# Split products for all wide input projections: halves of the activations kept, weights through two pairs of buffers

## The chip, the cores and the metric

One core of one Trainium2 chip runs the kernel. The metric is device time in microseconds, the median of several runs. The core has five engines: PE (matmul; its weight loads are shown apart as PEld), DVE (vector), ACT (scalar), POOL (GpSimd) and SP, which here only issues transfers.

## What is computed

One decoder layer on 512 tokens of width 1024, float32. Cut to what matters here:

```python
h = rmsnorm(x, g_pre_mix) * (1.0 + scale_m) + shift_m      # 512 x 1024
proj = h @ w_in                                            # one wide product, split by columns:
(gq, gk, gv, gg, ga_low, dq, dk, dv, iq, ik, iw, bg) = jnp.split(proj, offsets, axis=-1)
# widths 256 256 512 512 16 512 512 512 512 64 8 2048
o_a = gla_chunked(...gq, gk, gv, decay(ga_low)...)         # gated linear attention, silu(gg) on its output
o_b = dsa_attention(dq, dk, dv, top-128 keys by iq, ik, iw)
mix = sigmoid(bg[0]) * (o_a @ w_proj_gla) + sigmoid(bg[1]) * (o_b @ w_proj_dsa)
x   = x + gate_m * rmsnorm(mix @ w_out)
x   = x + gate_f * rmsnorm(hier_moe(h2))                   # 32 experts, top 2 of one group
```

## The kernel before, in words

The tokens lie in four tiles of 128 (`tt`), the width in eight blocks of 128 (`KD`). `hT` holds the transposed activations h in SBUF (8 blocks of 128 x 512). Each wide weight item is a block of 512 output columns, 2 MB, 128 x 4096 in SBUF. The list `items` gives their order: four `ada` items (conditioning), then IQ (index query), DK, DQ, DV, GQ (query and key of the linear attention, made transposed), GV, GG, BG, BG+D, proj 0, BG+512, BG+D+512, proj 1, out 0, out 1. SP loads them in that order (`load(n)`), into a ring of four buffers, item n once item n-4 is used up (with a few exceptions written out); PE counts used items in `ring_out`.

A product of one item and one token tile (`inproj`, L463) is eight fp32 matmuls of 128x512 into a PSUM bank A0 or A1; the trace records each as two instructions, so a product is sixteen. DK, the two proj items, BG+512, BG+D+512 and the two out items run already as split products (`inproj_split`, `split_matmul`, L471 to L473): ACT copies the float32 source to its high half in fp32r (`split_hi`, L1186), DVE subtracts to get the low half (`split_lo`, L1624), and PE does high x high, high x low and low x high, 24 matmuls for a product. The halves of h are made twice: once at the start for DK, into kv (high), gqk and qT (low), which are then overwritten (L1200, L1629), and once at the end of attention (`split_hi("h")`, L1832) for the late items. IQ, DQ, DV, GQ, GV, GG, BG and BG+D run in fp32 from `hT`.

Every engine works through its own list in program order, with semaphores between them:
- Start: `ada(0)`, then the narrow products `small` (L526, 88 columns) for four tiles, then IQ and DK, each with one `ada_step` (1 MB of conditioning weights through ACT's queue) per tile.
- Index stage, twelve steps n: PE does `index_scores(n)`; ACT the relu; DVE adds it up (L1686, L1688) and then does four rounds of the top-128 search (`some(4)`, L1664, L1665). In steps 3 to 6 and 8 to 11 PE also does one product each, of DQ and of DV.
- Attention stage, units u = 0 to 16: PE does `attn_scores(u)`, one product (GQ in u 0 to 3, GV, GG, BG four units each), and `attn_out(u-1)`: transposes (L592), ACT copies one half of them (L1347), DVE the other (L1821), and PE multiplies (L601). DVE masks the scores (L1797), in units 0 to 3 also finishes the search, and normalizes (L1806, L1807); ACT does the exponentials (L1332). From u = 8 on, the linear attention of chunk ch runs over an even unit (POOL L1066, DVE `gla_clamp` L1729, ACT `gla_exp` L1307 to L1311, DVE `gla_factors` L1736 and L1741, `gla_take` L1782, PE `gla_scores`) and the odd unit after it (PE `gla_out`, DVE `gla_norm` L1774).
- Then BG+D, `branches(0)`, BG+512, BG+D+512, `branches(1)`, the output product with the router, and 16 pairs of experts, whose weights SP loads into three sets of buffers.

Of the kernel before, what the change touches and what calls it, by code (L numbers as in the profile page):

```python
# [24 lines left out]
P = 128  # L25
# [55 lines left out]
def layer(nc, x, c, positions, w_ada, b_ada, g_pre_mix, g_post_mix, g_pre_ffn, g_post_ffn, w_in,  # L81
# [17 lines left out]
    with ExitStack() as ctx:  # L99
# [10 lines left out]
        def sem(name):  # L110
# [4 lines left out]
        ring = arena[:, 0:4 * 4096].rearrange("p (s n) -> p s n", s=4)  # L115
        hT = arena[:, 16384:20480].rearrange("p (k n) -> p k n", k=KD)
        prob = arena[:, 20480:22528].rearrange("p (b h n) -> p b h n", b=2, h=2)
        probT = arena[:, 22528:24576].rearrange("p (b h n) -> p b h n", b=2, h=2)
        adab = arena[:, 20480:24576].rearrange("p (b n) -> p b n", b=2)
        yc = arena[:, 0:8192].rearrange("p (t w n) -> p t w n", t=TT, w=2)  # L120
        wexp = arena[:, :].rearrange("p (s n) -> p s n", s=4)
# [6 lines left out]
        kv = sb("kv", [P, 4096])  # L128
        kT = kv[:, 0:2048].rearrange("p (c n) -> p c n", c=PAIRS)
# [25 lines left out]
        diag = stage_mem[:, 0:D]  # L155
        gla_mem = sb("gla_mem", [P, 3072])
# [78 lines left out]
        area_r["G"] = gvs_r[:, :]  # L235
        g_all, q_all = (v[:, :, :].rearrange("p a n -> p (a n)") for v in (gqk, qT))
        splits = {key: (area[raw], area_r[lo], area_r[hi]) for key, raw, lo, hi in (
            (("in", O_DK), 1, 1, 3), ("h", "H", "G", "B"), (("proj", 0), 1, 1, 3), (("in", O_BG + 512), 2, 2, "H"), (("in", O_BG + D + 512), 0, 0, 3),
            (("proj", 1), 1, 1, 2), (("out", 0), "H", "H", "B"), (("out", 1), 3, 3, "G"))}
        splits["g"], splits["q"] = (g_all, gqk_r[:, :], qi_r), (q_all, qT_r[:, :], stage_r)  # L240

        h_first = ([gqk_r[:, P * TT * k:P * TT * (k + 1)] for k in range(4)] + [qT_r[:, P * TT * k:P * TT * (k + 1)] for k in range(4)],
                   kv_r[:, :].rearrange("p (k n) -> p k n", k=KD))
        split_at = {key: n for n, key in enumerate(["h_first", ("in", O_DK), "h", ("proj", 0), "g", "q", ("in", O_BG + 512), ("in", O_BG + D + 512),
                                                    ("proj", 1), ("out", 0), ("out", 1)])}
# [17 lines left out]
        gu_sets = [[wexp[:, 2 * z + q, 0:4096] for q in range(2)] for z in range(2)] + [[gvs[:, :], qs_mem[:, :]]]  # L263
        down_sets = [[wexp[:, 2 * z + q, 4096:6144] for q in range(2)] for z in range(2)] + [[mk_mem[:, :], gla_mem[:, 0:2048]]]
# [91 lines left out]
        def slot_of(it):  # L356
            if it in splits:
                return splits[it][0]
            return ring[:, item_at[it] % 4, :]
# [15 lines left out]
        def _(pe):  # L375
# [52 lines left out]
            def ada_step(m):  # L428
# [7 lines left out]
                for j in range(4):  # L436
                    last = nc.tensor.matmul(o[32 * j:32 * j + 32, :], c32[:, k, :], adab[:, m % 2, j * 512:(j + 1) * 512],  # L437
                                            start=(k == 0), stop=(k == KD - 1))
# [16 lines left out]
            def inproj(it, tt):  # L455
# [6 lines left out]
                for k in range(KD):  # L462
                    last = nc.tensor.matmul(a[:, :], hT[:, k, tt * P:(tt + 1) * P], w[:, k, :], start=(k == 0), stop=(k == KD - 1))  # L463
# [11 lines left out]
            def split_wait(key):  # L475
                pe.wait_ge(hi_ready, split_at[key] + 1)
                pe.wait_ge(lo_ready, split_at[key] + 1)

            def inproj_split(it, tt):
                first = it == ("in", O_DK)  # L480
                split_wait("h_first" if first else "h")
                split_wait(it)
                w = parts(it, KD)

                def h(k):
                    hi, lo = (h_first[1][:, k, :], h_first[0][k]) if first else (v[:, k, :] for v in parts("h", KD))
                    return hi[:, tt * P:(tt + 1) * P], lo[:, tt * P:(tt + 1) * P]

                a, full = take_next("A", (it, tt))
                for k in range(KD):  # L490
                    last = split_matmul(a[:, :], h(k), [v[:, k, :] for v in w], k == 0, k == KD - 1)
                last.then_inc(full, 1)
                if tt == TT - 1:
                    pe.wait_ge(full, bank[where[(it, tt)]].at[(it, tt)] + 1)
                    pe.sem_inc(ring_out, 1)

            def inproj_T(it, cb):

                ring_wait(pe, it)
                a, full = take_next("A", (it, cb))  # L500
                w = slot_of(it).rearrange("p (k n) -> p k n", k=KD)
                for k in range(KD):
                    last = nc.tensor.matmul(a[:, :], w[:, k, cb * P:(cb + 1) * P], hT[:, k, :], start=(k == 0), stop=(k == KD - 1))  # L503
# [15 lines left out]

            pe.wait_ge(ld_small, 32)  # L520
            for tt in range(TT):
                a, full = take_next("A", ("small", tt))
                for k in range(KD):
                    if tt == 0:
                        pe.wait_ge(h_ready, k + 1)
                    last = nc.tensor.matmul(a[:, 0:NS], hT[:, k, tt * P:(tt + 1) * P], w_small[:, k, :], start=(k == 0), stop=(k == KD - 1))  # L526
                last.then_inc(full, 1)
            for tt in range(TT):
                inproj(("in", O_IQ), tt)
                ada_step(tt)  # L530
# [362 lines left out]
        def _(sp):  # L893
# [27 lines left out]
            for n in range(4):  # L921
                load(n)
            sp.dma_start(w_small[:, :, 0:RANK], win_v[:, :, O_GA:O_GA + RANK]).then_inc(ld_small, 16)
            sp.dma_start(w_small[:, :, RANK:NS], win_v[:, :, O_IK:O_IK + 72]).then_inc(ld_small, 16)
            load(4)
            load(5)
# [27 lines left out]

            sp.wait_ge(ring_out, item_at[("proj", 1)] + 1)
            experts(0, 0, 1)
# [4 lines left out]

            gate_up(2, 0, 4)
            down(2, 0, 4)
            sp.wait_ge(x1_ready, 2 * TT)
            gate_up(2, 1, 5)
# [182 lines left out]
        def _(act):  # L1148
# [34 lines left out]
            def split_hi(key):  # L1183

                src, _, hi = splits[key]
                nc.scalar.copy(hi, src).then_inc(hi_ready, 1)  # L1186


            def ada_load(m):
                act.dma_start(adab[:, m % 2, :], ada_v[:, m % KD, (1 + m // KD) * 2048:(2 + m // KD) * 2048]).then_inc(ada_in[m % 2], 16)  # L1190
# [3 lines left out]
            for tt in range(TT):  # L1194
                a, free = filled(act, ("small", tt))
                nc.scalar.copy(ikw[:, tt, :], a[:, 0:NS]).then_inc(ikw_in, 1)
                act.wait_ge(ikw_in, tt + 1)
                act.sem_inc(free, 1)
            act.wait_ge(h_ready, KD)
            nc.scalar.copy(h_first[1], hT).then_inc(hi_ready, 1)  # L1200
            act.wait_ge(ring_out, 4)
# [32 lines left out]
            for tt in range(TT):  # L1234
                to_stage((("in", O_IQ), tt))
                ada_next(tt + 2)
            act.wait_ge(lnv_ready, 1)
            nc.scalar.activation(st[:, 56:60], st[:, 52:56], ACT.Sqrt).then_inc(lnq_ready, 1)
            for tt in range(TT):
# [24 lines left out]
            for n in range(3 * PAIRS):  # L1264
# [19 lines left out]
                if n in WITH_PRODUCT:  # L1284
                    fill.pop(0)()

# [26 lines left out]
            gscr = stage_mem[:, 0:P]  # L1313
# [10 lines left out]
            for u in range(NU + 1):  # L1324
# [15 lines left out]
                if u:  # L1340
# [3 lines left out]
                    t, free = filled(act, ("p", v, 0))  # L1344
                    if v >= 2:
# [8 lines left out]
                if not odd and 0 <= ch < TT:  # L1354
# [5 lines left out]
                    act.sem_inc(free, 1)  # L1360
            scratch = gla_mem[:, 0:D]


            split_hi("h")
            sigmoid(0, 1, 0)
            act.wait_ge(ring_out, item_at[("in", O_BG)] + 1)
# [12 lines left out]
            act.wait_ge(ring_out, item_at[("in", O_BG + D)] + 1)  # L1379
            act.wait_ge(lo_ready, split_at["h"] + 1)  # L1380
            ring_wait(act, ("in", O_BG + 512))
            split_hi(("in", O_BG + 512))
            for ab, (used, key) in enumerate(((("proj", 0), ("in", O_BG + D + 512)), (("in", O_BG + 512), ("proj", 1)))):
# [755 lines left out]
```

## Time and profile before

| | |
|---|---|
| median of three runs | 894.28 us (892.54 to 897.63) |
| the profiled execution | 895.17 us, its span 893.4 us |
| PE busy | 760.0 us (85%), 3251 instructions |
| PEld, DVE, ACT, POOL busy | 408.1, 347.3, 257.7, 100.5 us |
| chain that ended last | PE 73%, DVE 11%, issue 7%, DMA 5%, ACT 3% |
| mean granted TensorE clock | 0.926 of 2.4 GHz |

A share of busy time says which engine has most to do over the whole span; the chain says what the end waited for, step by step. Both mix stages with different limits, so the rows below go stage by stage. In a table of stretches each row gives the length of the stretch, each engine's busy time (and number of instructions), the granted clock, the busy share of the DMA engines and GB/s. A line such as L1624 is the line of a helper that many steps share.

### The profile page before, as it was taken

Reading aid. Unit: us, or ns where it says so; the run is one execution under the profiler, and the core shown is the slowest. Engines: PE = TensorE matmul, PEld = TensorE weight load, DVE = VectorE, ACT = ScalarE, POOL = GpSimd, SP = SyncE. Lnnn points to the kernel's source line nnn. Section 1 sums busy time; section 2 is a strip of 40 time slices with the busy share of each in tenths; the row PEclk is TensorE's granted clock in tenths of the full one; section 3 lists DMA queues with packets and bytes.
Section 4 is the critical chain, followed back from the end, with each engine's and each line's share of the span. In section 5 each row is a group of like instructions: output and inputs, shape, how many; then the busy total and the mean of one; then the engine's idle time right before and its main releaser. Section 6 shows DMA issues by size and latency. Waiting matters only on the chain.

```text
span 893.4 us, 9183 instructions
## 1 busy us (share of the span) xinstructions
PE 760.0 (85%) x3251; PEld 408.1 (46%) x3251; DVE 347.3 (39%) x820; ACT 257.7 (29%) x479; POOL 100.5 (11%) x153
## 2 busy tenths in 40 slices
PE   2899989998899998989999989976998787787840
PEld 1554624343344554554578768852333232232310
DVE  3241024699733444536421374761522111112117
ACT  5031121432223554645212312313122121112123
POOL 3022201310000210100000000101010100101004
PEclk9879979999999989999999999976999898999985
DMA  9954483307022002000222235169799999999734
GB/s 344 376 192 141 142 311 113 102 1 282 16 79 94 1 1 95 1 1 1 94 95 95 94 139 238 48 264 398 285 421 421 420 421 420 417 421 421 323 123 184
DMA packets 45563, 179.48 MB, mean 201 GB/s; under 512 B 9567, under 2 KB 9673, under 8 KB 30157
## 3 DMA queue, kind: packets, MB, share of 16 engines
q1 hardware_dynamic: 37124, 149.48, 42.4%
q10 hardware_dynamic: 3464, 20.98, 6.6%
q0 software_dynamic: 4928, 8.42, 2.7%
q8 instruction: 27, 0.44, 0.2%
q14 instruction: 20, 0.16, 0.1%
HBM read 174.66 MB, written 12.59 MB: 210 GB/s over the span
## 4 chain that ended last, share of the span: by engine, by line
PE 73%; DVE 11%; issue 7%; DMA 5%; ACT 3%; SPq 0%; ACTq 0%; DVEq 0%; POOLq 0%; PEldq 0%
PE psA L463 19%; PE psG L842 7%; PE psS L842 7%; PE psA L863 6%; PE psA L471 6%; PE psA L473 5%; PE psA L472 5%; PE psT L829 2%; PE psA L526 2%; PE psO L437 2%; PE psO L601 1%; DVE mk_mem L1665 1%; DVE m L1664 1%; PE psS L582 1%; DMA xn_dram<-sig_mem 1%
## 5 line engine op out<-in xcount | busy, mean ns | idle before, releaser
L463 PE MATMUL psA<-arena 128*128 128x512 f32 x448 | 202.7, 607 | 0.0
L463 PEld LDWEIGHTS psA<-arena 128*128 128x128 f32 x448 | 84.8, 194 | 110.2 <-issue 110.2
L842 PE MATMUL psS<-arena,kv 128*64 128x512 f32 x192 | 50.4, 685 | 14.7 <-issue 14.7
L842 PE MATMUL psG<-arena,kv 128*64 128x512 f32 x160 | 39.9, 654 | 7.5 <-issue 7.5
L863 PE MATMUL psA<-arena,sig_mem 128*64 128x512 f32 x176 | 40.7, 605 | 0.5 <-ACT sig_mem L1490 0.5
L2060 DVE TENSOR_TENSOR sig_mem<-sig_mem,psS 128x256 f32<-128x256 f32 x8 | 4.9, 614 | 92.6 <-ACT sig_mem L1485 92.4
L1112 POOL DMA_INDIRECT y_dram<-sig_mem,tables x16 | 16.0, 1003 | 208.1 <-issue 134.4
L842 PEld LDWEIGHTS psS<-arena,kv 128*64 128x64 f32 x192 | 17.1, 156 | 46.9 <-issue 46.9
L1624 DVE TENSOR_TENSOR arena_r<-arena,arena_r 128x4096 fp32r<-128x4096 f32 x6 | 26.5, 4421 | 30.8 <-ACT arena_r L1186 30.8
L472 PE MATMUL psA<-arena_r,qs_mem_r 128*128 128x512 f32 x96 | 37.4, 389 | 0.0
L471 PE MATMUL psA<-arena_r,qs_mem_r 128*128 128x512 f32 x80 | 31.8, 398 | 3.5 <-DVEq L1855 2.7
L2060 DVE TENSOR_TENSOR sig_mem<-sig_mem,psG 128x256 f32<-128x256 f32 x8 | 4.9, 615 | 75.4 <-ACT sig_mem L1485 75.3
L1289 ACT ACTIVATE sig_mem<-psA 128x512 f32<-128x512 f32 x16 | 9.6, 597 | 76.3 <-PE psA L473 52.8
L1433 ACT ACTIVATE kv<-psT,shift,scale 128x128 f32<-128x128 f32 x64 | 24.1, 456 | 22.1 <-PE psT L829 22.1
L503 PE MATMUL psA<-arena 128*128 128x512 f32 x64 | 29.6, 616 | 0.0
L1874 DVE TENSOR_SCALAR kv<-psT,scale,shift 128x128 f32<-128x128 f32 x64 | 21.9, 404 | 19.4 <-PE psT L829 17.4
L842 PEld LDWEIGHTS psG<-arena,kv 128*64 128x64 f32 x160 | 13.7, 150 | 32.4 <-issue 31.5
L1664 DVE MAX8 m<-mk_mem 128x8 f32<-128x256 f32 (+2 forms) x48 | 26.9, 560 | 1.5
L1485 ACT ACTIVATE sig_mem<-psS 128x256 f32<-128x256 f32 x8 | 3.1, 384 | 84.4 <-PE psS L842 84.4
L601 PE MATMUL psO<-arena,kv 128*64 128x128 f32 x160 | 16.0, 284 | 12.0 <-ACT arena L1347 8.5
L1665 DVE MATCH_REPLACE8 mk_mem<-m,mk_mem 128x256 f32<-128x256 f32 (+2 forms) x48 | 26.0, 542 | 0.0
L829 PE MATMUL psT<-ident,kv 128*128 128x128 f32 x128 | 18.5, 292 | 8.8 <-DMA kv<-xn_dram,tables 8.8
(394 smaller groups left out, 1368.0 us busy)
## 6 DMA issues: line engine op xcount, KB each, us to landing
arena<-in_w_in_dram SPq DMA_DIRECT2D x11, 2048.0 KB, 10.4
arena<-in_w_e_gate_dram SPq DMA_DIRECT2D x22, 1024.0 KB, 24.8
arena<-in_w_e_up_dram SPq DMA_DIRECT2D x22, 1024.0 KB, 26.8
arena<-in_w_e_down_dram SPq DMA_DIRECT2D x22, 1024.0 KB, 20.6
arena<-in_w_ada_dram ACTq DMA_DIRECT2D x16, 1024.0 KB, 4.9
arena<-in_w_ada_dram SPq DMA_DIRECT2D x4, 2048.0 KB, 17.0
gvs<-in_w_e_gate_dram SPq DMA_DIRECT2D x5, 1024.0 KB
gvs<-in_w_e_up_dram SPq DMA_DIRECT2D x5, 1024.0 KB
```

Source lines behind the costliest of these rows:

```text
L463: last = nc.tensor.matmul(a[:, :], hT[:, k, tt * P:(tt + 1) * P], w[:, k, :], start=(k == 0), stop=(k == KD - 1))
L471: nc.tensor.matmul(acc, lhs[0], rhs[0], start=start, stop=False)
L472: nc.tensor.matmul(acc, lhs[0], rhs[1], start=False, stop=False)
L473: return nc.tensor.matmul(acc, lhs[1], rhs[0], start=False, stop=stop)
L503: last = nc.tensor.matmul(a[:, :], w[:, k, cb * P:(cb + 1) * P], hT[:, k, :], start=(k == 0), stop=(k == KD - 1))
L601: last = nc.tensor.matmul(o[64 * hh:64 * hh + 64, 0:P], val[:, kb, (2 * hp + hh) * HD:(2 * hp + hh + 1) * HD], probT[:, u % 2, hh, kb * P: ...
L829: last = nc.tensor.transpose(ps[name][:, q * P:(q + 1) * P], xg[:, b, k * P:(k + 1) * P], ident[:, :])
L842: last = nc.tensor.matmul(ps[g][64 * q:64 * q + 64, :].rearrange("p (g f) -> p g f", g=2), h2g[:, b, k, 64 * q:64 * q + 64], gu, start=(k ...
L863: last = nc.tensor.matmul(ps[name][64 * q:64 * q + 64, :], actT[:, b, kf, 64 * q:64 * q + 64], down_sets[z][q][:, D * kf + 512 * n:D * kf ...
L1624: V.tensor_tensor(lo, src, hi, ALU.subtract).then_inc(lo_ready, 1)
L1664: step(V.max(m8[:, :], work))
L1665: step(V.match_replace(work, m8[:, :], work, TAKEN))
```

## The change

IQ stays in fp32; the other wide items (DQ, DV, GQ, GV, GG, BG, BG+D besides those split before) run as split products. Its parts:

1. **h.** The raw `hT` moves to kv. Its halves are made once, `split_hi("h")` and `split_lo("h")`, into areas H and B of the arena, and stay there until BG+D+512 is done. The second split of h and the copies of the first in gqk, qT and kv are gone.
2. **Weights.** Items go in turn through two pairs of areas, (0, 1) and (3, 2): the raw item and then its low half in the first, the high half in the second. `load(n)` waits for n-1, so for the item two places before, which had the same pair. IQ has area 2, the ada items have 0, 1, H and B. out 0 goes to H and B, out 1 to 0 and 1.
3. **Splits in quarters.** DV, GQ, GV, GG, BG and BG+D are split in four pieces of 128x1024, put into the lists of ACT and DVE: for DV after steps 4 to 7 of the index stage, for GQ after steps 9 to 11, for the other four over the four units before their first product (ACT one, two, one and no piece; DVE none, one, two, one, at the end of the unit). ACT waits for the item's load before its first piece. PE waits piece by piece in the item's first product. DQ is split whole, after the index key is ready.
4. **Start.** SP loads IQ and DK before the narrow weights `w_small`. PE does IQ and its ada steps first and `small` after them; ACT copies the narrow results after IQ.
5. **Places.** `prob` moves to stage_mem, `probT` to the upper half of sig_mem, the two buffers of `ada_step` to qT and the upper half of gvs; the first expert sets get other areas. The first expert's gate and up weights are loaded before proj 1 is used up, and `gate_up(2, 1, 5)` before the wait for x1.

```diff
-        splits = {key: (area[raw], area_r[lo], area_r[hi]) for key, raw, lo, hi in (
-            (("in", O_DK), 1, 1, 3), ("h", "H", "G", "B"), (("proj", 0), 1, 1, 3), ...
+        split_order = [("in", O_DK), ("in", O_DQ), ("in", O_DV), ("in", O_GQ), ("in", O_GV), ("in", O_GG), ("in", O_BG), ("in", O_BG + D),
+                       ("proj", 0), ("in", O_BG + 512), ("in", O_BG + D + 512), ("proj", 1), ("out", 0), ("out", 1)]
+        home = {key: ((0, 1), (3, 2))[n % 2] for n, key in enumerate(split_order)}
+        home[("out", 0)], home[("out", 1)] = ("H", "B"), (0, 1)
+        splits = {key: (area[lo], area_r[lo], area_r[hi]) for key, (lo, hi) in home.items()}
+        splits["h"] = (kv[:, :], area_r["H"], area_r["B"])
+        hi_units, lo_units = ((0,), (1, 2), (3,), ()), ((), (0,), (1, 2), (3,))
+        hi_index = {4: [(dv, 0)], 5: [(dv, 1), (dv, 2)], 6: [(dv, 3)], 9: [(gq, 0), (gq, 1)], 10: [(gq, 2), (gq, 3)]}
+        lo_index = {5: [(dv, 0)], 6: [(dv, 1), (dv, 2)], 7: [(dv, 3)], 10: [(gq, 0)], 11: [(gq, 1), (gq, 2), (gq, 3)]}
...
             def inproj_split(it, tt):
...
                 for k in range(KD):
-                    last = split_matmul(a[:, :], h(k), [v[:, k, :] for v in w], k == 0, k == KD - 1)
+                    if tt == 0 and k % 2 == 0:
+                        split_wait(it, k // 2 + 1)
+                    last = split_matmul(a[:, :], [v[:, k, tt * P:(tt + 1) * P] for v in h], [v[:, k, :] for v in w], k == 0, k == KD - 1)
...
+            for tt in range(TT):
+                inproj(("in", O_IQ), tt)
+                ada_step(tt)
             pe.wait_ge(ld_small, 32)
...
-                    sp.wait_ge(ring_out, {7: 6, 8: 7, 9: 8, 15: 13, 16: 14, 17: 15, 18: 16}.get(n, n - 3))
+                    sp.wait_ge(ring_out, {4: 1, 5: 2, 6: 3, 18: 16}.get(n, n - 1))
...
+                for q in hi_units[u % 4] if u < NU else ():      # ACT, end of unit u
+                    key = in_units[u // 4]
+                    if q == 0:
+                        ring_wait(act, key)
+                    split_hi(key, q)
...
+                for q in lo_units[u % 4] if u < NU else ():      # DVE, end of unit u
+                    split_lo(in_units[u // 4], q)
```

## Rows read from the trace of the kernel before

**Rows 1.** The page: the chain that ended last, by engine.
```profile
PE 73%; DVE 11%; issue 7%; DMA 5%; ACT 3%; SPq 0%; ACTq 0%; DVEq 0%; POOLq 0%; PEldq 0%
```

**Rows 2.** Stretches: length, busy us of each engine, clock, DMA share, GB/s.
```profile
131.20:169.30 38.10, 37.53 (x130) 15.48 (x128) 16.68 (x45) 12.79 (x19) 7.39 (x17) 1.00 0.30 100
169.30:224.40 55.10, 51.22 (x144) 22.64 (x144) 51.26 (x136) 15.25 (x30) 8.30 (x15) 1.00 0.43 148
224.40:245.10 20.70, 18.82 (x54) 8.62 (x54) 15.74 (x47) 4.23 (x14) 0.00 (x0) 0.92 0.04 7
245.10:284.40 39.30, 35.83 (x127) 16.71 (x126) 10.13 (x44) 9.91 (x29) 0.00 (x0) 1.00 0.17 60
284.40:406.40 122.00, 112.09 (x575) 62.68 (x574) 56.69 (x168) 66.69 (x134) 15.32 (x17) 0.96 0.09 32
595.50:893.40 297.90, 215.91 (x967) 84.59 (x966) 72.78 (x164) 60.16 (x136) 41.72 (x36) 0.86 0.88 360
```

**Rows 3.** The chain of waits in order of time: start, us, what.
```profile
300.02 7.08 PE psA L463 x16
406.52 27.48 PE psA L463 x64
```

**Rows 4.** Order of time, ACT: copies behind split products in a row.
```profile
469.72 0.60 ACT L1289 ACTIVATE sig_mem<-psA 128x512 f32<-128x512 f32 x1 [1.04 <-PE psA L473]
475.16 0.60 ACT L1289 ACTIVATE sig_mem<-psA 128x512 f32<-128x512 f32 x1 [4.84 <-PE psA L473]
```

**Rows 5.** Groups by shape: busy us, mean ns, idle before. Whole splits.
```profile
L1186 ACT CAST arena_r<-arena 128x4096 fp32r<-128x4096 f32 x7 | 25.4, 3622 | 1.0 <-ACT sig_mem L1289 0.9
L1624 DVE TENSOR_TENSOR arena_r<-arena,arena_r 128x4096 fp32r<-128x4096 f32 x6 | 26.5, 4421 | 30.8 <-ACT arena_r L1186 30.8
```

**Rows 6.** Order of time, SP's queue at the start.
```profile
27.74 3.31 SPq L913 DMA_DIRECT2D arena<-in_w_in_dram  x2
```

**Rows 7.** Transfers issued from 27.0 to 28.6 us: KB, us to landing.
```profile
arena<-in_w_in_dram SPq DMA_DIRECT2D x1, 2048.0 KB, 10.9
```

**Rows 8.** The chain of waits: narrow products, first IQ, router products.
```profile
35.60 14.07 PE psA L526 x64
49.67 9.01 PE psA L463 x16
569.05 1.71 PE psG L741 x16
```

**Rows 9.** Stretches of one microsecond, columns as in Rows 2.
```profile
36.00:37.00 1.00, 1.00 (x6) 0.68 (x5) 1.00 (x3) 0.00 (x0) 0.00 (x0) 0.86 1.07 403
53.00:54.00 1.00, 1.00 (x3) 0.48 (x2) 0.30 (x1) 1.00 (x2) 0.00 (x0) 0.60 0.15 55
```

**Rows 10.** Order of time, DVE: the ends of a stretch without gaps.
```profile
169.37 1.30 DVE L1688 SCALAR_TENSOR_TENSOR mk_mem<-gqk,wi,mk_mem 128x384 f32<-128x384 f32 x2 [4.61 <-ACT gqk L1273]
...
224.10 0.28 DVE L1821 COPY arena<-psT 128x128 f32<-128x128 f32 x1
```

**Rows 11.** The chain of waits in an even unit and the odd one behind.
```profile
317.80 0.67 DVE gqk L1782
329.56 9.15 PE psA L463 x16
```

**Rows 12.** Order of time, ACT and DVE, beginning of that even unit.
```profile
309.79 1.28 ACT L1332 ACT_TABLE_LOAD   x1
310.26 0.56 DVE L1797 CUSTOM_DVE_ANT_0 arena<-psS,mk_mem 128x384 f32<-128x384 f32 x1 [1.93 <-PE psS L582]
311.17 0.61 ACT L1332 ACTIVATE arena<-arena,sm 128x384 f32<-128x384 f32 x1
```

**Rows 13.** Line L913: transfers of w_in, eleven issues.
```profile
DMA to landing us min/median/max: 7.6/10.4/20.4
```

**Rows 14.** Order of time, DVE, in the first branches products.
```profile
441.69 4.42 DVE L1624 TENSOR_TENSOR arena_r<-arena,arena_r 128x4096 fp32r<-128x4096 f32 x1
446.02 0.68 DVE L1854 TENSOR_TENSOR sig_mem<-psA,sig_mem 128x512 f32<-128x512 f32 x1
```

More of the change, by code:

```diff
@@ L497, in inproj_T @@
             def inproj_T(it, cb):
-                ring_wait(pe, it)
+                w, h = parts(it, KD), parts("h", KD)
                 a, full = take_next("A", (it, cb))
-                w = slot_of(it).rearrange("p (k n) -> p k n", k=KD)
                 for k in range(KD):
-                    last = nc.tensor.matmul(a[:, :], w[:, k, cb * P:(cb + 1) * P], hT[:, k, :], start=(k == 0), stop=(k == KD - 1))
+                    if cb == 0 and k % 2 == 0:
+                        split_wait(it, k // 2 + 1)
+                    last = split_matmul(a[:, :], [v[:, k, cb * P:(cb + 1) * P] for v in w], [v[:, k, :] for v in h], k == 0, k == KD - 1)
                 last.then_inc(full, 1)
@@ L952, in experts @@
                 down(z, 1, e1_)
+            gate_up(0, 0, 0)
             sp.wait_ge(ring_out, item_at[("proj", 1)] + 1)
-            experts(0, 0, 1)
+            gate_up(0, 1, 1)
+            down(0, 0, 0)
+            down(0, 1, 1)
             sp.wait_ge(ring_out, len(items))
@@ L1181, in _, with split_hi @@
             mod_row(0)
-            def split_hi(key):
+            def split_hi(key, q=None):
                 src, _, hi = splits[key]
-                nc.scalar.copy(hi, src).then_inc(hi_ready, 1)
+                part = slice(None) if q is None else slice(1024 * q, 1024 * (q + 1))
+                nc.scalar.copy(hi[:, part], src[:, part]).then_inc(hi_ready, 4 if q is None else 1)
             def ada_load(m):
-                act.dma_start(adab[:, m % 2, :], ada_v[:, m % KD, (1 + m // KD) * 2048:(2 + m // KD) * 2048]).then_inc(ada_in[m % 2], 16)
+                act.dma_start(adab[m % 2], ada_v[:, m % KD, (1 + m // KD) * 2048:(2 + m // KD) * 2048]).then_inc(ada_in[m % 2], 16)
             for m in range(2):
                 ada_load(m)
[L1194 to L1198, printed above, removed]
+            act.wait_ge(ring_out, 4)
             act.wait_ge(h_ready, KD)
-            nc.scalar.copy(h_first[1], hT).then_inc(hi_ready, 1)
-            act.wait_ge(ring_out, 4)
+            split_hi("h")
             ring_wait(act, ("in", O_DK))
@@ L1236, in _ @@
                 ada_next(tt + 2)
+            for tt in range(TT):
+                a, free = filled(act, ("small", tt))
+                nc.scalar.copy(ikw[:, tt, :], a[:, 0:NS]).then_inc(ikw_in, 1)
+                act.wait_ge(ikw_in, tt + 1)
+                act.sem_inc(free, 1)
             act.wait_ge(lnv_ready, 1)
             nc.scalar.activation(st[:, 56:60], st[:, 52:56], ACT.Sqrt).then_inc(lnq_ready, 1)
+            act.wait_ge(ring_out, item_at[("in", O_IQ)] + 1)
+            ring_wait(act, ("in", O_DQ))
+            split_hi(("in", O_DQ))
+            act.wait_ge(lo_ready, split_at["h"] + 4)
             for tt in range(TT):
@@ L1377, in _ @@
             sigmoid(0, 1, 3)
-            act.wait_ge(ring_out, item_at[("in", O_BG + D)] + 1)
-            act.wait_ge(lo_ready, split_at["h"] + 1)
             ring_wait(act, ("in", O_BG + 512))
             split_hi(("in", O_BG + 512))
-            for ab, (used, key) in enumerate(((("proj", 0), ("in", O_BG + D + 512)), (("in", O_BG + 512), ("proj", 1)))):
+            for ab, key in enumerate((("in", O_BG + D + 512), ("proj", 1))):
                 sigmoid(1, ab, 0)
-                act.wait_ge(ring_out, item_at[used] + 1)
                 ring_wait(act, key)
@@ L1716, in _ @@
                     mod_take(1 + n // 10)
+                for key, q in lo_index.get(n, ()):
+                    split_lo(key, q)
             dve.wait_ge(ld_ffn, 16 * 5)
```

98 lines of the change are left out of this document (40 added, 58 removed).

## The prediction

> **What bounds the kernel now.** I read the page first: the chain that ended last is PE for 73% of the span and DVE for 11% [rows 1]. That says only that PE is the usual bound, so I cut the span into stretches [rows 2] and asked of each which engine has no room. From 131.2 to 169.3 us (index stage, DQ) PE is busy 37.5 of 38.1 us: PE binds. From 169.3 to 224.4 (DV, first GQ) PE is busy 51.2 of 55.1 us, but DVE 51.3, and in order of time its instructions follow each other from 169.37 to 224.10 with nothing but the small steps between them [rows 10]: both are at their limit. From 224.4 to 245.1 DVE is busy 15.7 of 20.7. From 245.1 to 284.4 DVE has only 10.1 of 39.3: PE alone. From 284.4 to 406.4 no engine is full by itself; there the chain of waits goes around through DVE and ACT [rows 11]. From 406.4 PE runs BG+D without a gap [rows 3]. From 595.5 on the experts run with the DMA engines at 0.88 and 360 GB/s; nothing there changes in amount, so I take the end as moving with the start of that stretch.
>
> **One product.** In fp32 it is 7.08 us between other work and 27.48/4 = 6.87 in a row [rows 3]. A split product in a row takes 475.16 - 469.72 = 5.44 us [rows 4]; with other work between I take 5.51. So a product gains 1.57 us, or 1.43 in a row, at the full clock. Seven items of four products change: 28 x 1.57 = 44 us if nothing else limits. The split costs per item 3.62 us on ACT and 4.42 on DVE [rows 5]; in quarters I estimate 1.0 and 1.1 us. DVE's sum is 7 x 4.42 = 31 us, less some 4.4 us for the h split now made once, and it is what decides, stage by stage.
>
> **Start.** Before, the narrow products took 14.07 us at 35.60 and then IQ began with 9.01 us [rows 8], because the clock had gone to half at 36 us and came back only at 53 [rows 9]. The same kind of narrow product at the full clock is 1.71/16 = 107 ns each (router), against 14.07/64 = 220. IQ was issued at 27.74 and took 10.9 us, to 38.6 [rows 6, 7], behind the narrow weights; with those behind it I take it to land at about 36.3, bounds 35 to 38.6. IQ's dense work then sits at half clock and brings it back, and `small` after it runs at the full clock: 64 x 107 ns = 6.9 us. Gain 14.07 - 6.9 - 0.7 for the later IQ = 6.5 us, bounds 0 (all narrow products at half clock again) and 8.5 (the clock does not fall at all). The halves of h and DK need ACT twice 3.62 and DVE twice 4.42 us; they are ready near 54 us, and PE wants them near 77: hidden. So is DQ's split (8 us behind the narrow results, with over 30 us until its first product). If that cover went, each would cost its 8 us.
>
> **Index stage and units 0 to 3.** PE's four DQ products give 4 x 1.57 = 6.3 us, and DVE can follow, with its 16.7 busy of 38.1 us [rows 2] and three more pieces (3.3): its gapless run starts 5.8 us earlier in relation to DQ. From there DVE sets the pace: before, 169.4 to 245.1 is 75.7 us with 3.4 us of waiting; without the waiting and with nine pieces more (one of DV after step 7, four of GQ after steps 10 and 11, four of GV after units 1 to 3), 72.3 + 9.9 = 82.2 us, 6.5 more. Net loss 0.7, say 1 us: the 4 x 1.57 of DQ and also the eight products of DV and GQ are eaten. Bounds: +19 if the pieces found room (12 x 1.57), -5 if DVE also kept its old waits. PE's wait for a piece of DV or GQ falls into time in which it would wait for DVE anyway.
>
> **Units 4 to 7.** DVE 10.1 us of 39.3 plus four pieces, ACT 9.9 plus four: room. 4 x 1.57 = 6.3 us gained.
>
> **Units 8 to 15.** In the even unit u = 10 DVE's mask starts at 310.26, with PE's product [rows 12]; clamp, ACT's exponentials and DVE's factors follow, and `gla_take`, which frees the bank for PE, ends at 317.80 + 0.67 [rows 11]: 8.2 us, more than the 7.08 of the product beside it. So shortening that product gains nothing in units 10, 12 and 14; unit 8, which has no `gla_take`, gives 0.5. Worse, ACT has two pieces (2.1 us) at the end of units 9 and 13, ahead of the next unit's table load of 1.28 us at 309.79 and the exponential at 311.17, which had no room between them [rows 12]: +1.9 us each. Behind that waiting ACT are the factors, and behind them PE's transposes. In the odd units PE's product ends the unit, after DVE's normalizing: 4 x 1.57 = 6.3. DVE's own pieces at the end of units 9, 11, 13 and 15 (1.1 us each) fit into the 1.93 us that it waits ahead of the mask [rows 12], those of 10 and 14 under `gla_out`. Sum 6.3 + 0.5 - 3.8 = +3.0, bounds -4 and +13.
>
> **BG+D:** 4 x 1.43 = 5.7 us gained, in a row and with its pieces ready.
>
> **First branches.** BG+512 now may load only when BG+D is used up, at T. The shortest load is 7.6 us [rows 13]: T+7.7, ACT to T+11.4, DVE to T+15.9. DVE has that split in its list before `mixing(0,1)`, which frees the bank for PE's fifth half-product. Before, the split ran at 441.69 and the mixing at 446.02 [rows 14], which is T+12.0 with T = 434.0. Now it is T+15.9: 3.9 us lost, bounds 0 and 8 (load of 11.5). The loads of BG+D+512, proj 1, out 0 and out 1 have four products or more before them (21.8 us against 16): 0. The two places where expert weights come earlier change nothing that the chain waits for: 0.
>
> **The clock.** PE now idles more where DVE or ACT leads. The odd unit at 329.56 shows what it costs: 9.15 us for a product of 7.08 [rows 11], with the clock at 0.96 over the whole of the linear attention [rows 2]. I take one and a half such events more: -3 us, bounds 0 and -17. By itself: the Trainium skill, TensorE: Matmul & The Clock Gate, section on HAM oscillation, says that waits between bursts of matmuls throw the clock back, so that each burst starts cold again; it speaks against this change, and by it the clock rival below would hold. The trace agrees in one place in four here.
>
> **Sum.** 6.5 - 1 + 6.3 + 3.0 + 5.7 - 3.9 - 3 = 13.6 us off the profiled execution's 895.17 (span 893.4 and 1.8 around it), so 881.6. The median of the runs stood 0.9 below that execution: 880.7, say 881.
>
> **The rivals.**
> - *DVE's pieces find room.* The pieces go where DVE waits, and DV and GQ gain too: 12 x 1.57 = 18.8 instead of -1, time 861. For it: DVE is idle 21 us between 131.2 and 169.3 [rows 2]. Against: only two and a half items' pieces could be put there, and the run from 169.4 has no gap.
> - *The clock.* Each of the eight units of linear attention loses the 2.07 us of the product at 329.56: 8 x 2.07 = 17 instead of 3, so 895. For: rows 11. Against: before, most of its units kept the full clock.
> - *ACT stands at a load (slower).* ACT waits for an item's load at the end of the unit after the pair came free. PE needs about 9 us to there, a load 7.6, so it just fits. The median landing is 10.4 and the longest 20.4 [rows 13]; from 9 us on ACT holds up its own exponentials, DVE behind them and PE. At 14 us, 5 us for each of GV, GG, BG, BG+D and 3 for BG+512, with the softmax chain restarted each time: 22 us, time 903. Against: after 171 us the DMA engines are nearly idle, 0.04 to 0.17 in units 1 to 16 [rows 2].
> - *The start gives nothing*, because the narrow products stay slow behind IQ: 887.5.
>
> **How the numbers follow.** Forecast as worked out 0.54; DVE finds room 0.13; clock 0.14; ACT at the loads 0.10; start 0.09. A measurement of this kernel tells 0.5% (4.5 us) from no change. Faster than 889.8: 0.54 + 0.13 + 0.09 and 0.01 of the clock case, 0.77; within: 0.12; slower: 0.11. Range 867 to 894: it leaves out the far ends of the first and third rivals.
>
> **What would show it.** Right: from DQ's first product to `attn_scores(4)` 115 us, about as before (245.1 - 131.2 = 113.9), with DVE busy over 90% and PE some 20 us less; units 4 to 7 near 7.9 us each; even units 10 and 14 longer than 12; PE's wait before its fifth half-product in `branches(0)` at about 5 us; narrow products near 7 us behind IQ. Wrong: narrow products at 14 us, clock under 0.9 in units 8 to 16, ACT idle for a DMA at the end of units 0, 4, 8 or 12, or a start of the experts that does not move the end.

## The result, and the profile after

The changed kernel takes 906.35 us (median of four runs: 902.3, 905.3, 907.4 and one of 1219.4 at a granted clock of 0.557, a slow run that the ratio leaves out) against 895.45 before. The ratio is 1.0124, 95% interval 1.0096 to 1.0151; on a second chip it was 1.0119 (1.0064 to 1.0174). The forecast was 881 us, with a range up to 894. It went the other way.

The page of the changed kernel (span 905.7, before 893.4): the chain that ended last, by engine. It answers to [rows 1].

```profile
PE 65%; DVE 15%; issue 8%; DMA 6%; ACT 5%; SPq 0%; ACTq 0%; DVEq 0%; POOLq 0%; PEldq 0%
```

Stretches of the changed kernel (length, busy us of PE, PE's loads, DVE, ACT, POOL, clock, DMA share, GB/s). The first three stand for the second to fourth of [rows 2], cut at nearly the same points of the program; 274.10:416.00 is units 8 to 15 with their tail; the last lies as the fifth of [rows 2] does.

```profile
157.10:217.20 60.10, 48.59 (x192) 34.84 (x192) 56.22 (x141) 20.00 (x35) 7.88 (x15) 0.88 0.18 55
218.00:239.10 21.10, 16.66 (x71) 12.40 (x70) 19.24 (x51) 7.08 (x17) 0.00 (x0) 0.82 0.18 61
239.10:274.10 35.00, 31.53 (x155) 23.56 (x154) 14.78 (x49) 13.52 (x32) 0.00 (x0) 0.94 0.09 28
274.10:416.00 141.90, 125.95 (x640) 93.50 (x640) 69.00 (x177) 72.89 (x142) 15.38 (x17) 0.76 0.12 44
284.40:406.40 122.00, 110.79 (x546) 82.76 (x544) 56.47 (x151) 64.48 (x125) 12.21 (x15) 0.72 0.05 18
```

In the last row, over the same 122 us, PE is as busy as before (110.8 us, 112.1 before), but at a mean clock of 0.72 instead of 0.96. PE's busy time hides it: work that has become shorter takes as long because more of it runs at half clock. Cut where the clock changes, units 8 to 15 of the changed kernel hold four stretches at half clock, 68.4 us in all:

```profile
284.40:294.70 10.30, 10.30 (x61) 7.83 (x59) 4.25 (x15) 5.74 (x16) 2.08 (x3) 0.50 0.00 0
311.70:332.20 20.50, 19.53 (x87) 14.15 (x88) 9.18 (x24) 8.22 (x20) 4.02 (x5) 0.50 0.00 0
349.30:366.40 17.10, 17.10 (x79) 12.65 (x80) 5.09 (x15) 7.42 (x18) 3.89 (x5) 0.50 0.01 1
383.40:403.90 20.50, 19.73 (x86) 14.65 (x87) 8.60 (x22) 8.72 (x19) 0.00 (x0) 0.50 0.00 1
```

The kernel before has two, 10.3 us in all, in units 9 and 11:

```profile
296.10:299.60 3.50, 3.50 (x16) 2.22 (x16) 2.72 (x10) 1.24 (x4) 0.16 (x1) 0.51 0.00 0
326.90:333.70 6.80, 6.80 (x19) 3.58 (x18) 2.88 (x9) 3.98 (x12) 4.00 (x5) 0.50 0.00 0
```

The two traces can be laid side by side by the start of PE's scores in each unit. What each stretch took, before and after, in us (gain: time saved):

| stretch | before | after | gain | forecast |
|---|---|---|---|---|
| start, to the first index scores | 114.61 | 106.32 | +8.3 | +6.5 |
| index stage, units 0 to 3 | 130.5 | 132.8 | -2.3 | -1 |
| units 4 to 7 | 38.5 | 35.0 | +3.5 | +6.3 |
| units 8 to 15, to BG+D's first product | 122.9 | 142.8 | -19.9 | +3.0, and -3 for the clock |
| BG+D | 27.5 | 21.9 | +5.6 | +5.7 |
| first branches | 24.1 | 31.2 | -7.1 | -3.9 |
| the rest | 435.3 | 435.6 | -0.3 | 0 |

Four of the seven are near, two are off by about 3 us. One, off by 20, turned the result.

How it happens shows in the chain of waits of unit 10 and the odd unit behind it, in the changed kernel (start, us, what; `...` stands for lines left out):

```profile
302.49 2.00 ACT arena_r L1189 x2
304.50 1.28 ACT L1342
309.47 2.37 DVE qs_mem L1748 x6
311.84 0.61 DVE gqk L1789
...
321.99 0.72 PE psG L633 x2
322.71 0.72 PE psO L632 x2
...
328.10 0.73 PE psA L476
328.83 0.43 PE psA L477
...
332.52 0.23 PE psA L477
```

ACT's two pieces (2.00) stand ahead of its table load, then come the exponentials, DVE's factors and `gla_take`. PE is through with its short product and the transposes behind it by 309.4 and then waits for `gla_take`, until 312.64. What it does next, the end of the even unit, runs at half clock:

```profile
286.00:290.00 4.00, 4.00 (x34) 3.32 (x32) 0.80 (x2) 2.32 (x2) 0.00 (x0) 0.50 0.00 0
312.60:320.00 7.40, 7.33 (x51) 5.97 (x53) 0.64 (x2) 2.97 (x4) 0.00 (x0) 0.50 0.00 0
```

The first row is the same place in unit 8. These are the 32 small matmuls of `gla_scores` (L617), a pair of them 0.21 us at half clock and 0.11 at the full one. Then the odd unit: in unit 11 the pairs of `gla_out` (L632, L633) take 0.72 us where they take 0.42 at the full clock, and the product behind them starts with 0.43 for a matmul that takes 0.23 from 332.52 on. All four pairs of units have such a stretch in the changed kernel. Before, unit 11 had one [rows 11], which began only in the last two pairs of `gla_out`, and unit 9 had a short one that was over with its `gla_out`; units 12 to 15 had none. PE's waits from 284 to 410 us (us in total, times, longest), changed kernel:

```profile
PE psT L592 <- DVEq L1791: 8.7, 3, 3.3
PE psO L601 <- ACT sig_mem L1359: 2.1, 4, 0.8
```

The first was 2.6 us in four waits, at most 0.8, before.

### The profile page after: what moved, and what is told of

Same layout as the page of the kernel before. It is cut to its first block, busy times and chain, and to the rows that moved or that the text cites. A ratio compares the mean times of both kernels' runs of the same rounds, so it can differ in the third digit from the quotient of the medians.

```text
span 905.7 us, 9686 instructions
## 1 busy us (share of the span) xinstructions
PE 749.1 (83%) x3475; PEld 469.7 (52%) x3475; DVE 377.4 (42%) x843; ACT 280.5 (31%) x503; POOL 105.3 (12%) x153
## 4 chain that ended last, share of the span: by engine, by line
PE 65%; DVE 15%; issue 8%; DMA 6%; ACT 5%; SPq 0%; ACTq 0%; DVEq 0%; POOLq 0%; PEldq 0%
PE psA L476 9%; PE psA L477 8%; PE psA L478 8%; PE psG L842 7%; PE psS L842 7%; PE psA L863 6%; PE psA L468 3%; DVE mk_mem L1670 3%; DVE m L1669 2%; PE psT L829 2%; DMA arena<-in_w_in_dram 2%; PE psO L601 2%; PE psG L617 2%; PE psO L440 1%; PE psS L582 1%
## 5 line engine op out<-in xcount | busy, mean ns | idle before, releaser
L476 PE MATMUL psA<-arena_r 128*128 128x512 f32 x320 | 135.0, 422 | 4.9 <-DVE arena_r L1636 4.3
L477 PE MATMUL psA<-arena_r 128*128 128x512 f32 x320 | 130.3, 407 | 0.0
L478 PE MATMUL psA<-arena_r 128*128 128x512 f32 x320 | 129.7, 405 | 0.0
L1636 DVE TENSOR_TENSOR arena_r<-arena,arena_r 128x1024 fp32r<-128x1024 f32 (+1 forms) x32 | 64.7, 2040 | 48.9 <-ACT arena_r L1189 46.9
L476 PEld LDWEIGHTS psA<-arena_r 128*128 128x128 f32 x320 | 63.9, 200 | 33.1 <-issue 18.9
L842 PE MATMUL psS<-arena,kv 128*64 128x512 f32 x208 | 68.0, 690 | 13.6 <-issue 13.6
L478 PEld LDWEIGHTS psA<-arena_r 128*128 128x128 f32 x320 | 63.4, 198 | 14.3
L477 PEld LDWEIGHTS psA<-arena_r 128*128 128x128 f32 x320 | 64.0, 200 | 12.9 <-issue 0.2
L842 PE MATMUL psG<-arena,kv 128*64 128x512 f32 x208 | 61.4, 619 | 6.8 <-issue 6.8
L1189 ACT CAST arena_r<-arena 128x1024 fp32r<-128x1024 f32 (+1 forms) x32 | 53.5, 1692 | 26.6 <-DMA arena<-in_w_in_dram 14.0
L476 PE MATMUL psA<-arena_r,qs_mem_r 128*128 128x512 f32 x96 | 39.5, 411 | 7.9 <-DVEq L1858 7.1
L477 PE MATMUL psA<-arena_r,qs_mem_r 128*128 128x512 f32 x96 | 38.5, 401 | 0.0
L863 PE MATMUL psA<-qs_mem,sig_mem 128*64 128x512 f32 x80 | 36.5, 598 | 0.5 <-ACT sig_mem L1501 0.5
L601 PE MATMUL psO<-sig_mem,kv 128*64 128x128 f32 x160 | 19.5, 323 | 19.2 <-DVE sig_mem L1830 9.8
L842 PE MATMUL psS<-gvs,kv 128*64 128x512 f32 x48 | 25.7, 697 | 8.2 <-issue 8.2
L1444 ACT ACTIVATE kv<-psT,shift,scale 128x128 f32<-128x128 f32 x64 | 24.1, 457 | 23.0 <-PE psT L829 23.0
```

The costliest lines, as they stand in the source:

```text
L476: nc.tensor.matmul(acc, lhs[0], rhs[0], start=start, stop=False)
L477: nc.tensor.matmul(acc, lhs[0], rhs[1], start=False, stop=False)
L478: return nc.tensor.matmul(acc, lhs[1], rhs[0], start=False, stop=stop)
L601: last = nc.tensor.matmul(o[64 * hh:64 * hh + 64, 0:P], val[:, kb, (2 * hp + hh) * HD:(2 * hp + hh + 1) * HD], probT[:, u % 2, hh, kb * P: ...
L842: last = nc.tensor.matmul(ps[g][64 * q:64 * q + 64, :].rearrange("p (g f) -> p g f", g=2), h2g[:, b, k, 64 * q:64 * q + 64], gu, start=(k ...
L863: last = nc.tensor.matmul(ps[name][64 * q:64 * q + 64, :], actT[:, b, kf, 64 * q:64 * q + 64], down_sets[z][q][:, D * kf + 512 * n:D * kf ...
```

## The experiments

Beside the time stand two readings of the profiled run: the stretch from unit 8's scores to BG+D's first product, and the mean clock of the window 284.4 to 406.4. The window is fixed in time and does not hold quite the same work in each run. Each of these two is one execution, and they vary: "even" and "even and branch order" run the same program in units 8 to 15 and read 121.1 and 123.3 us, clock 0.96 and 0.93.

| kernel | ratio to before (95%) | units 8 to 15, us | clock |
|---|---|---|---|
| before | 1 | 122.9 | 0.96 |
| changed | 1.0119 (1.0064, 1.0174) | 139.9 and 142.8 | 0.75 and 0.72 |
| before, short products | 1.0141 (1.0112, 1.0171) | 133.3 | 0.79 |
| before, new start | 0.9947 (0.9921, 0.9972) | 122.9 | 0.96 |
| changed, 8 added in all | 1.0058 (1.0018, 1.0097) | 132.0 | 0.92 |
| changed, 8 added in even | 0.9941 (0.9911, 0.9971) | 121.1 | 0.96 |
| changed, branch order | 1.0081 (1.0046, 1.0117) | 142.8 | 0.72 |
| even and branch order | 0.9877 (0.982, 0.9934) | 123.3 | 0.93 |
| changed, pieces one a unit | 1.0184 (1.0142, 1.0225) | 144.6 | 0.76 |
| even, branch, one a unit | 0.9875 (0.9822, 0.9928) | 129.8 | 0.90 |
| the same with 4 added | 1.0059 (1.0027, 1.009) | 137.2 | 0.82 |
| even, branch, pieces 1-1-2-0 | 0.9825 (0.9767, 0.9883) | 119.4 | 0.96 |
| even with 12, branch | 0.985 (0.9795, 0.9905) | 123.0 | 0.96 |

Many of the intervals overlap, of the last six rows above all; where rows with overlapping intervals are told apart, it is by the trace.

**1. Short products in the kernel before: is it the clock alone?** Two of the eight blocks of k are left out of each GG and BG product. No halves of these weights are made, on no engine, as in the kernel before.

```diff
-                for k in range(KD):
-                    last = nc.tensor.matmul(a[:, :], hT[:, k, tt * P:(tt + 1) * P], w[:, k, :], start=(k == 0), stop=(k == KD - 1))
+                kn = KD - 2 if it in (("in", O_GG), ("in", O_BG)) else KD
+                for k in range(kn):
+                    last = nc.tensor.matmul(a[:, :], hT[:, k, tt * P:(tt + 1) * P], w[:, k, :], start=(k == 0), stop=(k == kn - 1))
```

> The kernel before, with two of the eight blocks of k left out of each product of units 8 to 15 (GG and BG), which then take 5.3 us, as long as split ones, with no split work on ACT and DVE. It leaves out a quarter of these eight products. Theory 1 (the clock): the granted clock of these units, 0.96 before, falls to 0.85 or below by the shorter PE work alone, and the time does not fall, or rises: 893 to 903. Theory 2 (the pieces): no piece lengthens a chain here, the four odd units give 1.77 each, the clock stays: 888.

Measured: 906.85 us, ratio 1.0141. Eight products are shortened by some 1.7 us each (7.08 to 5.36 at the full clock), 14 us of PE work is left out, and the stretch is 10.4 us longer. Its window, and its chain in unit 11:

```profile
284.40:406.40 122.00, 107.51 (x493) 63.87 (x492) 53.85 (x160) 61.90 (x129) 13.62 (x16) 0.79 0.10 35
```

```profile
305.73 5.36 PE psA L464 x12
...
328.96 0.72 PE psG L634 x2
329.68 0.72 PE psO L633 x2
...
335.08 7.28 PE psA L464 x12
```

The same six matmuls (twelve instructions in the trace) take 5.36 us in unit 9 and 7.28 in unit 11, behind `gla_out` at 0.72 a pair. Cut at the changes of the clock, this kernel has four stretches at half clock in these units, 51 us in all, where the kernel before has 10.3. Shorter products alone, with no split work, make this kernel slower. The rival, that the pieces do it, is not needed for that.

**2. The changed kernel with PE filled up again.** Eight matmuls are put ahead of each product and overwritten by the first that counts. At 0.23 us each they take about what the split saves (1.8 against 1.6 us):

```diff
+                    if k == 0 and it in (("in", O_GG), ("in", O_BG)) and tt % 2 == 0:
+                        for _ in range(8):
+                            nc.tensor.matmul(a[:, :], h[0][:, 0, tt * P:(tt + 1) * P], w[0][:, 0, :], start=True, stop=True)
```

In all eight units (without `tt % 2`):

> The changed kernel with eight more matmuls of 128x512 at the head of each product of units 8 to 15 (GG and BG), into the same bank, overwritten by the first one that counts: they only keep PE busy for about 1.7 us a unit. Theory 1 (the clock, borne out by the kernel before with shortened products, 906.9): the clock of these units comes back to 0.95 or more and units 8 to 16 take about 12 us less, some 895. Theory 2 (the pieces of the splits lengthen the chain in the changed kernel, and the clock only follows): the time stays at 906 or rises to 913.

In the four even ones, where PE waits anyway:

> The same, with the eight added matmuls in units 8, 10, 12 and 14 only, where PE waits for the chain of DVE and ACT anyway. If PE's idle time in the even units is what throws the clock back, this does as much as the version with all eight and saves the 1.7 us of each odd unit: 889 to 892. If the clock wants PE full in all units, it lies between the changed kernel and the version with all eight: 898 to 903.

Measured: 898.05 (ratio 1.0058; its ten runs spread from 892.5 to 905.8) and 889.85 (0.9941). More PE work, less time: the second adds 32 matmuls to the changed kernel and takes 1.8% less, by the ratios to the kernel before. The version with the even units only:

```profile
284.40:406.40 122.00, 109.50 (x679) 82.40 (x677) 65.38 (x166) 69.91 (x135) 15.50 (x17) 0.96 0.10 35
```

```profile
PE psT L595 <- DVEq L1794: 3.9, 4, 1.5
```

The clock is back at 0.96 and the stretch at 121.1 us, below the 122.9 of before, with every piece of the splits in it. Of half clock 10.2 us are left, all in unit 11. That is the decisive pair: 142.8 - 121.1 = 21.7 us of the changed kernel's stretch are the clock, and the shorter odd products pay for the pieces. How far single executions vary shows when the other profiled runs of the same units are paired: 139.9 - 123.3 = 16.6 is the least. The ratios tell of 0.9941 against 1.0119, some 16 us for the whole kernel.

**3. The start alone, in the kernel before.** IQ and DK loaded ahead of the narrow weights, IQ's products ahead of the narrow ones, all in fp32.

```diff
+            for tt in range(TT):
+                inproj(("in", O_IQ), tt)
+                ada_step(tt)
             for tt in range(TT):
...
-                inproj(("in", O_IQ), tt)
-                ada_step(tt)
```

> The kernel before with only the reordering of the start: IQ and DK are loaded ahead of the narrow weights, PE runs IQ ahead of the narrow products; all fp32. If the gain of 8.3 us at the start of the changed kernel comes from the order alone (the narrow products at the full clock, 7 us for 64 instead of 14), it is kept to the end: 887. Rival: it came with the split of DK or is given back behind the index stage, where DVE sets the pace: 895.

Measured: 888.77 against 893.3, ratio 0.9947: 4.5 us, where I expected some 7. Its profiled run has the narrow products at 7.31 us (before 14.07 [rows 8]) and reaches the first index scores at 108.61, 6.0 us early, with IQ's first product at 8.83 us because the clock still fell (0.63 from 36 to 40 us). The gain is the order's, not the split's.

**4. DVE's order in the first branches.**

```diff
-            after = {(0, 0): ("in", O_BG + 512), (0, 3): ("in", O_BG + D + 512), (1, 1): ("out", 0), (1, 2): ("out", 1)}
+            after = {(0, 1): ("in", O_BG + 512), (0, 3): ("in", O_BG + D + 512), (1, 1): ("out", 0), (1, 2): ("out", 1)}
```

> The changed kernel, with DVE's low halves of BG+512 in its list behind mixing(0,1) instead of mixing(0,0). The prediction's term: DVE's wait for this split is what holds the bank for PE's fifth half-product in branches(0), 3.9 us predicted, some 7 lost there with the clock's fall. Mixing(0,1) frees the bank first, so 5 to 6 us come back: 901. Rival: PE then waits for the low halves themselves (they are needed by the first product of branches(1) only), or the clock was the loss: 905 to 906.

> Both: the added matmuls in the even units of 8 to 15 and the low halves of BG+512 behind mixing(0,1). If the two losses are independent they add: 884 to 887, ahead of the kernel before. If the clock after unit 15 carried a part of the loss of the first branches, the sum is 2 to 3 us smaller: 888.

Order of time in the changed kernel, ACT, DVE and PE (start, us, idle before and what ended it):

```profile
447.07 3.63 ACT L1189 CAST arena_r<-arena 128x4096 fp32r<-128x4096 f32 x1 [7.71 <-DMA arena<-in_w_in_dram]
450.80 4.42 DVE L1636 TENSOR_TENSOR arena_r<-arena,arena_r 128x4096 fp32r<-128x4096 f32 x1 [4.33 <-ACT arena_r L1189]
455.14 0.68 DVE L1857 TENSOR_TENSOR sig_mem<-psA,sig_mem 128x512 f32<-128x512 f32 x1
456.03 0.76 PE L476 MATMUL psA<-arena_r,qs_mem_r 128*128 128x512 f32 x1 [5.76 <-DVEq L1858]
```

In the version with the other order, DVE:

```profile
451.18 0.69 DVE L1857 TENSOR_TENSOR sig_mem<-psA,sig_mem 128x512 f32<-128x512 f32 x1 [2.03 <-PE psA L478]
452.02 0.69 DVE L1861 TENSOR_TENSOR kv<-sig_mem 128x512 f32<-128x512 f32 x1
452.63 4.42 DVE L1636 TENSOR_TENSOR arena_r<-arena,arena_r 128x4096 fp32r<-128x4096 f32 x1
```

The mixing that frees the bank now stands ahead of the split; PE's longest wait there goes from 5.76 to 1.34 us, and from 436 to 456 us PE is busy 19.6 instead of 13.9. Ratios 1.0081 (changed: 1.0124 and 1.0119) and, with the even units filled, 0.9877 (0.9941 without): 3.4 to 5.7 us, with intervals that overlap. The profiled runs settle it: all six versions with this order take 23.9 to 24.0 us for the first branches, the five without it 29.7 to 31.2. The two gains add, within what the runs can tell: 882.67 us with both, ahead of both kernels.

**5. ACT's pieces.** That version kept two stretches at half clock, 3.4 us in unit 9 and 13.6 us from unit 10 into unit 11, the second behind ACT's two pieces on the chain. First one piece to a unit:

```diff
-        hi_units, lo_units = ((0,), (1, 2), (3,), ()), ((), (0,), (1, 2), (3,))
+        hi_units, lo_units = ((0,), (1,), (2,), (3,)), ((), (0,), (1,), (2, 3))
```

> The changed kernel, with ACT's four pieces of an item one to a unit (0, 1, 2, 3) instead of 1, 2, 1, 0, and DVE's behind them (0, 1, 1, 2). The prediction's term: two pieces on ACT at the end of units 9 and 13 stand 2.0 us ahead of the next unit's table load and exponentials, on the chain. If the term holds, units 10 and 14 are 1 us shorter each, and PE's wait in them, which throws the clock back, is too: 3 us against the changed kernel, 902. If only PE's shorter products count for the clock: 905. Rival: ACT's piece in the even units, and DVE's two at the end of the odd ones, cost as much as is gained: 906.

> All three: the added matmuls in the even units of 8 to 15, the low halves of BG+512 behind mixing(0,1), ACT's pieces one to a unit. The version with the first two had one stretch at half clock left, from 318 us, behind the chain of unit 10 that ACT's two pieces open (302.30, 2.00 us). If they go, 1 us of the chain and 3 to 5 of the half clock go: 877 to 879. If the half clock comes anyway: 881 to 883.

Measured: 909.84 (1.0184), slower than the changed kernel, and 888.97 (ratio 0.9875, five runs from 881.4 to 896.4; the median is only 0.4% under the kernel before on its chip), no better than without. Both expectations failed. DVE in the first one, at the end of unit 7 and the start of unit 8:

```profile
276.92 1.23 DVE L1636 TENSOR_TENSOR arena_r<-arena,arena_r 128x1024 fp32r<-128x1024 f32 x1 [0.83 <-ACT arena_r L1189]
278.06 0.55 DVE L1806 CUSTOM_DVE_ANT_0 qs_mem<-psS,mk_mem 128x384 f32<-128x384 f32 x1
```

DVE waits 0.83 us for ACT's piece and then does its second one, both ahead of the mask, which comes 2.7 us after unit 8's scores (275.35), where in the changed kernel on that chip it came 1.0 after them (275.39 and 274.44). The edit had moved the cost from ACT's end of an odd unit to DVE's. So next the second piece of ACT went to the end of the even unit, DVE's as they were:

```diff
+        hi_units, lo_units = ((0,), (1,), (2, 3), ()), ((), (0,), (1, 2), (3,))
```

> The version with the added matmuls in the even units and the low halves of BG+512 behind mixing(0,1), with ACT's pieces as 1, 1, 2, 0 instead of 1, 2, 1, 0 in the four units of an item, DVE's unchanged (0, 1, 2, 1). The second of ACT's two pieces at the end of units 9 and 13, ahead of the next table load, goes to the end of units 10 and 14, under gla_out; DVE waits for none at the end of an odd unit (what cost 2.7 us in unit 8 with the pieces one to a unit). If the chain of unit 10 is ACT's, 1 us there and some of the half clock in unit 11 go: 879 to 881. If the half clock is PE's idle time whatever ACT does: 882 to 883.

Measured: 879.57 us against 896.24 on its chip, 0.9825, the lowest ratio of all, though its interval overlaps those of the versions near it. Its window, and PE's wait for `gla_take`:

```profile
284.40:406.40 122.00, 111.59 (x686) 84.12 (x685) 63.87 (x163) 71.87 (x134) 15.54 (x17) 0.96 0.10 35
```

```profile
PE psT L595 <- DVEq L1794: 2.2, 4, 0.6
```

Unit 10 takes 14.08 us instead of 14.96 with the pieces as they were and the same filling, unit 14 14.75 instead of 15.62: 0.9 us for each piece of 1.0. The version with twelve added, which has the pieces as they were, reads 14.98 and 15.68 there. Unit 11 begins at the full clock, but `gla_out` still ends at 0.72 a pair.

**6. How much filling.** Four matmuls in each even unit (on top of the version with pieces one to a unit), and twelve:

> The same with four added matmuls instead of eight in each even unit. If what matters is that PE is busy, half the filling gives back a part of it: the clock of units 8 to 15 between 0.72 and 0.93, the time 3 to 10 us above the version with eight. If any filling will do: the same time, or up to 1 us less.

> The same two edits with twelve added matmuls instead of eight in each even unit, ACT's pieces as in the changed kernel. Product and filling are then 5.5 + 2.6 = 8.1 us, as long as the chain of 8.2. If more filling keeps the clock up in unit 11 as well (0.79 from 320 to 340 us with eight), 3 to 5 us come off: 878 to 880. If eight are enough and the rest is PE time on the path: 884 to 886.

Measured: four 1.0059, clock 0.82; twelve 0.985, clock 0.96, the stretch 123.0 us. With its pieces one to a unit this kernel has 0.76 without filling and 0.90 with eight, so half the filling gave less than half of the clock back (one execution each), and most of the time is lost again. Twelve give no time in the stretch (123.0, with eight 121.1 and 123.3) and a clock of 0.96, which eight reached too. Unit by unit, twelve leave units 10 and 14 as they are with eight and make units 8 and 12 0.9 us longer, which is the four more matmuls at 0.23: in those two units filling of this length is no longer covered by a wait.

> The changed kernel as it is, beside the three others on one chip, so that they can be compared with it directly. Both theories: 1.012 of the kernel before, as first measured, 904 to 907.

Measured: 902.61, ratio 1.0119.

## Why the prediction was wrong, step by step

**The step that failed** is *The clock*: "I take one and a half such events more: -3 us, bounds 0 and -17". It cost 21.7 us by the pair of experiment 2 (16.6 at the least, some 16 by the ratios): five to seven times the term, at or beyond the far end of its bounds. The rival that I priced at 17 and gave 0.14 was the mechanism (its time of 895 lay outside the stated range already, which I had not noticed: the prediction names only the first and the third rival as left out): in the even units PE idles under a chain of 8.2 us, and each idle stretch is paid at its end and in the odd unit behind it. The mistake was in what I took from [rows 11]. I priced the event by its product, 9.15 - 7.08 = 2.07 us, and left out what else can run at half clock: `gla_out` ahead of it, in the changed kernel eight pairs at 0.72 instead of 0.42, 2.4 us more, and the scores at the end of the even unit. Unit by unit, against the version with the even units filled, the changed kernel loses 2.1, 2.7, 2.2 and 3.1 us in the even units and 2.0, 0.4, 4.5 and 4.9 in the odd ones (unit 11's is small because that version keeps its event there). And I counted events by how many the old kernel had, one place in four, when the change shortens just that PE work with which the others had none. The count itself was short: the trace before has a second, smaller event in unit 9, which [rows 11] do not show. "So shortening that product gains nothing in units 10, 12 and 14" was the sentence to stop at: by the prediction's own numbers PE's idle time there grows by 1.6 us each. What I held against the rival, that most units before kept the full clock, held only with the long products (experiment 1).

The Trainium skill, TensorE: Matmul & The Clock Gate, section on HAM oscillation, gave this direction, and I had cited it beside the forecast. Its waits are for transfers, those here are for DVE and ACT; here the trace agrees, 0.96 to 0.72.

**Units 8 to 15, without the clock**, were right in mechanism. The version with the even units filled shows what the clock hides: even units 0.4, 1.3, 0.2 and 1.1 us longer than before, odd ones 2.2, 0.05, 1.3 and 1.1 shorter, +1.8 in all; forecast +3.0. Not all of that is free of the clock and the filling: unit 9 also gains about 0.9 in `gla_out`, which ran at half clock before, unit 11 keeps its event in both, and in units 8 and 12 product and filling (5.5 + 1.8 us) are longer than the 7.08 of before. ACT's two pieces ahead of the table load (1.9 us each forecast) are the row at 302.49, 2.00 us; units 10 and 14 are 1.3 and 1.1 longer, and moving one of the two pieces gave 0.9 back in each.

**First branches**, -3.9 forecast, -7.1 measured: the mechanism is the rows under experiment 4: ACT starts at T+8.2 (forecast 7.7 for the load), then DVE, then the mixing. The fifth half-product came at T+17.2 where it had been at T+12.9 (T = 438.85 and 434.0), 4.3 us. The rest is the clock again, which I had not added: 0.76 for its first matmul instead of 0.47, and half clock up to 461.9:

```profile
455.10:461.90 6.80, 5.87 (x14) 4.64 (x15) 2.42 (x5) 0.00 (x0) 0.00 (x0) 0.50 0.01 2
```

**Start**, +8.3 for +6.5, right: 7.31 us for the 64 narrow products (6.9 forecast), in this chain of the changed kernel:

```profile
36.09 7.13 PE psA L468 x16
...
68.62 7.31 PE psA L529 x64
```

The rest over the forecast is IQ's first product: in this execution it ran at the full clock from 36 us, for which I had allowed as the upper bound; in that of experiment 3 it took 8.83. The size is one execution's: all eleven profiled versions of the changed kernel have this start and reach the first index scores at 105.9 to 110.4 us, a gain of 4.2 to 8.7, in the mean 6.7.

**Index stage and units 0 to 3**, -2.3 for -1, right: 116.2 us from DQ's first product (122.84) to `attn_scores(4)` (239.08), 115 forecast; DVE is busy 56.2 of 60.1 us and PE 48.6. All eight products of DV and GQ were eaten, as forecast. That DVE sets the pace is read, not tested: no run took its pieces away.

**Units 4 to 7**, +3.5 for +6.3: three units gain 1.4 each, as forecast in size (1.57); unit 4 loses 0.7, and it begins at half clock:

```profile
239.10:243.00 3.90, 3.90 (x12) 2.67 (x12) 2.80 (x11) 1.47 (x5) 0.00 (x0) 0.50 0.58 215
```

PE had idled in the stretch before it (16.7 busy of 21.1, clock 0.82). **BG+D**, +5.6 for +5.7, and the experts, 0 for 0: right.

**ACT stands at a load**: not in the units. ACT waited for w_in in three places, 14.0 us in all, of which 7.71 are the one before `branches` that I had in the forecast.

Left open: what the pieces cost with the clock held in each single unit. No run leaves the halves out of the changed kernel's units 8 to 15, so their cost is told by the sums above, and only the move of one of ACT's pieces is measured by itself.

## What to carry to other kernels

Before work is taken off TensorE in a stretch that another engine's chain bounds, look at the granted clock of that stretch and at what follows: in this kernel the idle time there was not free, it was paid at half clock by the next matmuls, small ones included, and the price of an event was everything that ran until the clock was back. Where the product can't be made to matter, leave it long, or fill the wait with matmuls whose result is thrown away: here 32 of them took 1.8% off the changed kernel's time. And when one piece of work is moved off a chain, see which engine's list it enters before the next step that others wait for.

## What was not expected of the hardware

The mean clock of the window answered by degrees to the filling (within it the clock is at one of two levels, and the stretches at half clock grow shorter or fewer): with ACT's pieces as in the changed kernel, 0, 8 and 12 added matmuls in each even unit gave 0.72 to 0.75, 0.93 to 0.96 and 0.96 over the same window; with one piece to a unit, 0, 4 and 8 gave 0.76, 0.82 and 0.90. Filling all eight units did worse than the four (132.0 us and clock 0.92 against 121.1 and 0.96), by more than the four times 1.8 us of PE time that it adds, although its profiled run was one of its fastest. Its trace has half clock from 311.8 to 328.9 and from 386.9 to 390.3, in units 10, 11 and 15; why there, no run here tells. That version's ten runs go from 892.5 to 905.8 us, and the time goes with the clock: the three slowest have a mean clock of 0.902 to 0.904, the others 0.909 to 0.922. The kernel before had 889.3 to 901.2 us on the same chip.
